# Residual update on VectorE in the joins of a diffusion backbone, with the normalised slices issued one at a time

## The reference

```python
xl = xl + mod_l[2] * rmsnorm(yl, mix_post_g[i])          # residual update behind the token mixer
hl = modulate(rmsnorm(xl, ffn_pre_g[i]), mod_l[3], mod_l[4])   # input of the feed-forward part
xl = xl + mod_l[5] * rmsnorm(swiglu(hl, ffn_w13[i], ffn_w2[i]), ffn_post_g[i])
```

## Time and profile before

| | us |
|---|---|
| median of 3 runs | 2299.72 (2298.67 to 2301.72) |
| the profiled execution, its own time | 2299.72 |
| span of its trace | 2297.9 |
| PE busy | 2119.7 (92%) |
| DVE busy | 1137.2 (49%) |
| ACT busy | 864.0 (38%) |
| POOL busy | 171.6 (7%) |
| L673, residual update on POOL, 49 instructions | 51.0 |
| mean granted TensorE clock | 0.947 of full speed |

### The profile page before, as it was taken

How to read it: one execution, slowest core, us unless ns; L and a number is a source line. 1 busy time by engine, 2 the same in 40 slices (tenths; PEclk the granted TensorE clock), 3 DMA queues, 4 the chain that set the end, 5 groups by cost and what they waited for, 6 DMA issues and landing times.

```text
span 2297.9 us, 31537 instructions
## 1 busy us (share of the span) xinstructions
PE 2119.7 (92%) x13233; PEld 1656.1 (72%) x13233; DVE 1137.2 (49%) x1892; ACT 864.0 (38%) x1416; POOL 171.6 (7%) x234
## 2 busy tenths in 40 slices
PE   4999989899999999998999999998748899998998
PEld 2755556687777767754557778886747799977997
DVE  2322453635556566645253555664392545536454
ACT  2442223533333353321243333335533544525444
POOL 0000000302101121010011200011000000000000
PEclk8999799999999999999999999999559999999999
DMA  6334241445544555432145653344632455424553
GB/s 250 128 135 167 92 150 53 138 149 159 176 150 163 185 173 206 178 127 103 37 147 175 205 196 133 115 142 167 220 147 92 128 185 184 128 85 151 183 183 108
DMA packets 228682, 344.23 MB, mean 150 GB/s; under 512 B 9238, under 2 KB 192321, under 8 KB 226300
## 3 DMA queue, kind: packets, MB, share of 16 engines
q1 hardware_dynamic: 218016, 313.41, 39.5%
q0 software_dynamic: 9808, 28.53, 4.1%
q10 hardware_dynamic: 716, 0.26, 0.0%
HBM read 319.76 MB, written 26.61 MB: 151 GB/s over the span
## 4 chain that ended last, share of the span: by engine, by line
PE 85%; DVE 9%; DMA 2%; ACT 2%; issue 1%; SPq 0%; ACTq 0%; DVEq 0%
PE bank L960 20%; PE bank L961 20%; PE bank L962 20%; PE bank L397 4%; PE bank L826 4%; PE bank L871 2%; PE bank L1712 1%; PE bank L1348 1%; PE bank L2412 1%; DMA arena<-mod_w 1%; PE bank L637 1%; PE bank L2045 1%; PE bank L627 1%; PE bank L1324 1%; DVE h_lo L733 1%; DVE w_lo L922 1%
## 5 line engine op out<-in xcount | busy, mean ns | idle before, releaser
L960 PE MATMUL bank<-h_hi,w_hi 128*128 128x512 f32 (+1 forms) x1480 | 512.5, 346 | 12.6 <-DVE h_lo L733 11.9
L961 PE MATMUL bank<-h_lo,w_hi 128*128 128x512 f32 (+1 forms) x1480 | 504.8, 341 | 0.0
L962 PE MATMUL bank<-h_hi,w_lo 128*128 128x512 f32 (+1 forms) x1480 | 504.5, 341 | 0.0
L922 DVE TENSOR_TENSOR w_lo<-ring,w_hi 128x1024 fp32r<-128x1024 f32 (+1 forms) x282 | 323.9, 1185 | 313.4 <-ACT w_hi L917 313.4
L960 PEld LDWEIGHTS bank<-h_hi,w_hi 128*128 128x128 f32 x1480 | 282.9, 191 | 53.2 <-DVE h_lo L733 15.9
L917 ACT ACTIVATE w_hi<-ring 128x1024 fp32r<-128x1024 f32 (+1 forms) x282 | 274.0, 1019 | 106.0 <-PE bank L962 102.6
L962 PEld LDWEIGHTS bank<-h_hi,w_lo 128*128 128x128 f32 x1480 | 283.0, 191 | 32.2 <-issue 0.2
L961 PEld LDWEIGHTS bank<-h_lo,w_hi 128*128 128x128 f32 x1480 | 283.4, 191 | 29.1 <-issue 0.2
L960 PE MATMUL bank<-g_hi,w_hi 128*128 128x512 f32 (+1 forms) x704 | 241.3, 343 | 0.0
L961 PE MATMUL bank<-g_lo,w_hi 128*128 128x512 f32 (+1 forms) x704 | 237.0, 337 | 0.0
L962 PE MATMUL bank<-g_hi,w_lo 128*128 128x512 f32 (+1 forms) x704 | 236.7, 336 | 0.0
(11 more groups left out here) (323 smaller groups left out, 2965.3 us busy)
## 6 DMA issues: line engine op xcount, KB each, us to landing
ring<-ffn_w SPq DMA_DIRECT2D x120, 1024.0 KB, 5.1
mod_ring<-mod_w SPq DMA_DIRECT2D x88, 1024.0 KB, 7.1
ring<-ffn_w SPq DMA_DIRECT2D x16, 768.0 KB, 4.6
ring<-hy_w_in SPq DMA_DIRECT2D x12, 1024.0 KB, 5.3
arena<-mod_w SPq DMA_DIRECT2D x8, 1024.0 KB, 17.1
s_in_weights<-arena POOLq DMA_DIRECT2D x32, 256.0 KB, 3.1
s_out_weights<-arena POOLq DMA_DIRECT2D x16, 512.0 KB, 4.8
ring<-s_w_glu SPq DMA_DIRECT2D x8, 1024.0 KB, 5.8
```

What stands on the lines that cost most here:

```text
L922: nc.vector.tensor_tensor(self.lo[:, i % SPLIT, a:b], self.w.slot(i)[:, a:b], self.hi[:, i % SPLIT, a:b].bitcast(F32), ALU.subtract).then_ ...
L960: nc.tensor.matmul(o, w[0], v[0], start=first, stop=False)
L961: nc.tensor.matmul(o, w[0], v[1], start=False, stop=False)
L962: return nc.tensor.matmul(o, w[1], v[0], start=False, stop=last)
```

## The change

`Join.gpsimd` is removed: DVE does the residual update of every slice. The run-ahead of DVE is taken out of the loop: pass k issues `normed(k)`, then `scaled(k+1)` and `update(k+1)`, then `remainder(k)`. Before the loop stand `scaled(0)`, `update(0)`, `scaled(1)`, `update(1)`. `update` waits for the semaphore of the `scaled` right in front of it. Half (0,0) moves from the place ahead of `scaled(0)` to the place behind `normed(0)`; half (1,1) moves from behind `remainder(3)` to behind `remainder(2)`, next to half (0,1). On ACT the rounding of half (1,1) moves from ahead of the first shift to behind slice 1. No arithmetic is added or removed.

```diff
-            def gpsimd(self, pool):
-
-                if self.post and self.pre:
-                    n = self.n
-                    for k in range(1, KD):
-                        pool.wait_ge(*self.t.after(k + 1))
-                        nc.gpsimd.tensor_tensor(x[:, k, 0:n], x[:, k, 0:n], Y[:, k, 0:n], ALU.add).then_inc(x_updated, 1)
...
                     self.first.round(act, 1, 0)
-                    if self.parts:
-                        self.first.round(act, 1, 1)
...
                         nc.scalar.activation(h_hi[:, k, 0:self.n], SQ[:, k, 0:self.n], ACT.Copy).then_inc(h_rounded, 1)
+                        if k == 1:
+                            self.first.round(act, 1, 1)
...
+                    dve.wait_ge(*self.spreads.after(1))
+                    scaled(0)
                 else:
...
-                if self.first:
-                    self.first.remain(dve, 0, 0)
-                if self.post:
-                    dve.wait_ge(*self.spreads.after(1))
-                scaled(0)
...
-                update(0)
-                scaled(1)
+                if self.post:
+                    update(0)
+                    scaled(1)
+                    update(1)
                 dve.wait_ge(*self.spreads.after(2 if self.post else 1))
-                normed(0)
-
                 for k in range(KD):
-                    scaled(k + 2)
-                    normed(k + 1)
+                    normed(k)
+                    if k == 0 and self.first:
+                        self.first.remain(dve, 0, 0)
+                    if self.post and k:
+                        scaled(k + 1)
+                        update(k + 1)
                     if self.parts:
                         remainder(k)
                         if k == 0:
                             self.first.remain(dve, 1, 0)
-                        if k in (2, 3):
-                            self.first.remain(dve, k - 2, 1)
+                        if k == 2:
+                            self.first.remain(dve, 0, 1)
+                            self.first.remain(dve, 1, 1)
```

More of the change, by code:

```diff
@@ L716, in scaled @@
                 def scaled(k):
-                    if self.post and k < KD:
+                    if k < KD:
                         nc.vector.tensor_tensor(Y[:, k, 0:n], Y[:, k, 0:n], bank[5][:, 0:n], ALU.mult).then_inc(j_step, 1)
                 def update(k):
-                    if self.post and k < KD:
+                    if k < KD:
                         dve.wait_ge(*self.t.after(k + 1))
@@ L725, in normed @@
                 def normed(k):
-                    if k < KD:
-                        if self.post:
-                            dve.wait_ge(*self.x.after(k + 1))
-                        nc.vector.tensor_tensor(SQ[:, k, 0:n], x[:, k, 0:n], bank[4][:, 0:n], ALU.mult).then_inc(x_normed, 1)
+                    if self.post:
+                        dve.wait_ge(*self.x.after(k + 1))
+                    nc.vector.tensor_tensor(SQ[:, k, 0:n], x[:, k, 0:n], bank[4][:, 0:n], ALU.mult).then_inc(x_normed, 1)
                 def remainder(k):
```

## The result

The changed kernel takes 2322.49 us (median of 4 runs, 2320.32 to 2325.91), the kernel before 2299.19 in the runs beside it (4 runs, 2298.29 to 2301.72): ratio 1.0101, 95% interval 1.0084 to 1.0118. It is slower by 23.3 us. The profiled execution took 2329.59 us, with a span of 2327.8 and a mean granted clock of 0.944 (before: 0.947). It lies 7 us above its kernel's median, so the two traces differ by 29.9 us of span, and part of that is not the change's own. (Four later runs of the same changed kernel gave a median of 2326.43; the figure moves by some us from one set of runs to the next.)

The account below looks back on a forecast made before the run. PE, 92% busy and 85% of the chain, bounds the kernel; the DVE-ACT round trip becomes the lead-ins' bound. 13.2 + 5.8 + 3.4 + 1.0 + 1.8 = 25.2 on 2299.7 gives 2325 us, range 2315 to 2337.

Parts of the forecast that it names:

- the trip: Split joins: a slice's way DVE to ACT and back, 2.57 us, plus a 0.60 step sets a 3.17 pace.
- the three joins with 512 tokens: Behind attention, ahead of and behind Hyena: PE ends 4.4 us later in each, +13.2 in all.
- First join: Reciprocal 0.84 us sooner, but slices paced by the round trip; PE ends at 79.8 against 74.02, +5.8.
- Two with 256: Split joins with 256 tokens: round trip 1.60 us, step 0.34; +1.7 each, twice +3.4.
- Ahead of S5: Unsplit join: DVE's pass becomes 1.97 us against ACT's 1.32 for a slice; +1.0.
- FNet: Join ahead of FNet: DVE's copies stand behind the join and PE waits for the first copy; +1.8.
- The half (0,0): 512-token joins: its new place gains nothing, since DVE waits for PE's spread there anyway.
- PE at each slice: Joins: PE waits for h_lo at each slice, starts 3.17 us apart (1.94 with 256 tokens), 5.4 at slice 3.
- The clock: Rival, chance 0.14: gaps in the joins put PE at 1.2 GHz; +11, 2336 us.
- Behind each join the delays add up: Behind joins: PE's order is unchanged and PE is nearly the whole chain, so delays summed to 25.2 us.
- The self-wait: DVE's scaled ahead of a waiting update charged 0.71 us, not 0.60; by the skill's rule, sum about 1.5 less.
- The lock: DVE and GpSimd's shared port: POOL's additions delay DVE 0.72 us each; time given back left out of the sum.

Follow-up runs that it names:

- The instruction inside: Changed kernel plus one unread vector multiply between update and remainder in slices 1 to 6 of five split joins: 2326.03 us, ratio 1.0109.
- the same one outside: Changed kernel plus the same unread vector multiply, placed behind the remainder and ahead of the next normed: 2339.33 us, ratio 1.0162.
- the kernel with the additions alone: Kernel before with POOL's residual additions put on DVE, run-ahead kept: 2302.19 us, ratio 1.0017.
- the one with the tables later: Changed kernel with GpSimd's memsets ahead of its loads and two large Hyena tables held until the eighth bank's eviction: 2319.68 us, ratio 1.0092.

## Why the prediction was right, and where not

**The cause** held: the trip, not the work in it. The instruction inside cost nothing, the same one outside its whole length. Taking the run-ahead out alone costs 21.8 us in the joins, and giving it back to the changed kernel takes away 18.9 of its 24.0.

**The terms.** Predicted 13.2 for the three joins with 512 tokens, measured 12.5. The trip is 2.50 and not 2.57, since the 2.57 that I took held for slice 0 alone. Behind attention `normed(0)` to `h_lo(7)` takes 27.76 and not 28.18; `normed(0)` comes 0.06 later and PE's end 0.1 later than reckoned, which leaves the 0.3 that this join is short. First join: 5.8 and 5.5 (6.8 if counted from its length in the kernel with the additions alone, where its order is the same as before). Two with 256: 3.4 and 2.5; the trip is 1.54 instead of 1.60. Ahead of S5: 1.0, and 1.1 to 2.4 over the profiles with this order. FNet: 1.8 and 2.3. Each pass of DVE took 1.24 there and not 1.16, and PE waited for the first copy:

```profile
2053.93 3.72 PE L2513 MATMUL bank<-arena,h_sb 128*128 128x256 f32 x16 [2.54 <-DVE arena L2532]
```

Sum: 25.2 and 24.0.

**The half (0,0)** was said to gain nothing in the joins with 512 tokens. In the changed kernel that is so. I did not see that the place it left was the cheap one: it costs as soon as the run-ahead is back.

**PE at each slice** depends on the clock. Ahead of Hyena PE stops at each slice from 3 on, with starts 3.12 apart, as forecast. Behind attention there is one gap, ahead of slice 3, with a half-speed stretch behind it that hides the rest. DVE idles 0.50 ahead of `h_lo` and not 0.7, since the trip is 0.07 shorter and the update there takes 0.69 and not 0.54.

**The clock** as a rival was half right. It did fall behind the long gap, but I priced it as if every delay of PE added up, +11. PE has 0.38 to spare in each slice against DVE's 3.11, and pays nearly all of the 1.3 back before the join ends.

**"Behind each join the delays add up"** is the step that did not hold everywhere. In the feed-forward stages it does: each is as long in all traces within 0.03 us. In the Hyena stage a load is triggered by the last `h_lo`, and what counts is its distance from the end of the lead-in, 5.5 before and 3.0 after. I had looked at the weight panels' transfers only, and not at POOL's tables, which start at the same event. That is 2.2 at the third group and 3.7 at the fourth, outside the sum. That the median still came out 2.5 below the forecast is partly luck: the scatter of the clock is larger than these terms.

**The self-wait** of the update: `scaled` to update is 0.72 here (441.78 to 442.50), where 0.54 to 0.60 separates instructions that do not wait for one another. The Trainium skill, "VectorE: DVE Perf Modes", section "The DRAIN you can't avoid", has this for nothing; the rows say 0.1 again at full width. It reached PE only ahead of S5 and FNet.

**The lock** on the port that the prediction weighed agrees with the rows: before, 15 of the 32 full-width remainders were 1.4 long, and with the additions off POOL all are 0.69. It was worth nothing here. In the kernel with the additions alone the joins with 512 tokens did not shorten (0.0 to 0.2 longer): DVE has the additions themselves in exchange, and PE ends those joins.

## What to carry to other kernels

Where a slice goes from one engine to another and back, its pace is here the length of that trip plus the last step, whatever stands inside as long as it fits, unless the next slice's first step is issued ahead of this one's last. Count what fits inside the trip before moving work there, and look for the place where the engine waits for a third one: that is the free place. When a join's end moves against its last producer, look at every load that this producer triggers, on all queues together.

## What the runs showed that I had not expected

The same work runs at different granted clocks in different executions. Windows of 20 us in attention, PE's busy time with its count of matmuls, granted clock, DMA share and GB/s, in the changed kernel and in the one with the tables later, whose attention stage is the same code:

```profile
200.50:220.50 20.00, 20.00 (x110) 1.00 0.59 211
220.50:240.50 20.00, 18.02 (x69) 0.82 0.33 106
240.50:260.50 20.00, 18.93 (x68) 0.58 0.12 32
```

```profile
199.40:219.40 20.00, 20.00 (x110) 1.00 0.58 211
219.40:239.40 20.00, 17.71 (x82) 1.00 0.33 106
239.40:259.40 20.00, 18.93 (x129) 1.00 0.32 106
```

PE's busy time ahead of the fall is the same (20.00 of 20 us), and in the one execution the clock fell there and in the other only in the window behind those shown (0.73). Why, I can't say. The attention stage took 332.6 to 343.2 us over the 13 traces, the trace before being the longest of them. Feed-forward stages repeat within 0.03 us, and joins with the same order within 0.4, except the first join and the one ahead of S5, which vary by up to 1.4. A change of a few us is better read from the lengths of its own stretches than from the total.

About 4.2 MB of loads behind the Hyena lead-in, 1.0 each for the panel and the modulation weights and 2.2 of tables, land together: issuing one of them 3.9 us sooner made it land 0.4 sooner, and holding back 1.5 MB took away the wait.
